# A SwiGLU feed-forward that multiplies its input before the norm factor is known: the factor is applied to the gate and up sums of the first half of the tokens

## The chip, the cores and the metric

The kernel runs on one core of a Trainium2 chip. The time is the device time of one execution in microseconds (us); several executions are timed and the median is taken. One execution more is recorded by the hardware profiler, and the rows in this document come from it. A core has five engines that run their own instruction streams and meet only at semaphores: TensorE (PE, with its weight loads listed as PEld), VectorE (DVE), ScalarE (ACT), GpSimd (POOL) and SyncE (SP), which here only issues DMAs.

## What is computed

The reference is one layer of a decoder with 1,024 prompt tokens and 8 × 4 sample tokens, so 1,056 tokens of width 1,024. What matters here is its end:

```
x = x + (sig(gA) * (A @ w_a) + sig(gB) * (Bn @ w_b)) @ w_o      # the merge; call the new x "x1"
gate, up = split(rmsnorm(x1, g_ffn) @ w_ffn_in)                  # 1024 -> 2 x 2816
x = x1 + (silu(gate) * up) @ w_ffn_out
```

The norm is `rmsnorm(x)[t, d] = x[t, d] * r[t] * g[d]`, where `r[t]` is one over the root of the token's mean square (plus 1e-6). The factor `r[t]` is the same for every channel of a token, so it can be taken out of the product: `gate[t] = r[t] * ((x1 * g) @ w)[t]`, and the same for up.

## The kernel before, in words

Activations lie transposed in SBUF: channels on the 128 partitions, tokens along the free dimension. `x1` is a tile of 8 channel blocks × 1,056 tokens. Every large product is made from three products of rounded parts: a weight block is cast to its high part on ACT (`w_h`), DVE subtracts that from the raw weights (`w_l`), the operand is split in the same way, and `split_product` (L84 to L91) multiplies low × high, high × low and high × high into the same PSUM banks. Each stage is a block of code that all engines leave together: no engine enters the next block before the last one has left the old one.

**The merge** (`stage_merge`, L2423). Its last product, `y @ w_o`, runs in 8 tiles of 128 output channels, each of two weight blocks. Between the two blocks PE transposes the old x for the tile (L2703) from `x_rows`, which POOL has loaded by DMA in four column groups (L2543, L2544) before the product starts. ACT copies the transposed x into `x1` (L2606), DVE adds the product (L2659), ACT squares the tile (`square_tile`, L2600) and POOL adds the squares over the tiles (L2550). ACT and DVE also cast and subtract the weight blocks of the next tile (`split`, L2560, L2622), SP loads them. Behind the last tile stands a chain: ACT squares tile 7, POOL adds it, PE multiplies the sums with a matrix of ones so that every partition has the total of its token (L2709, three pieces of 352 tokens in plain f32), DVE makes the mean square (L2662), ACT the root (L2614), DVE the reciprocal (L2665). That is `k.rs`, the factor r for all 1,056 tokens.

**The feed-forward** (`stage_ffn`, L2712) takes the tokens in two halves of 528. A half has 22 pairs of blocks, gate f and up f (each 8 channel blocks × 6 matmuls of 264 tokens = 48 matmuls), and then 24 blocks of the down product. Weights go raw (three buffers) → `w_h` (ACT, L2830) → `w_l` (DVE, L2890), prepared two blocks ahead (`LEAD`), three deep (`NSPLIT`). At the start of the first half DVE makes each channel block `h2 = x1 * g * r` (`h2_tile`, L2901), ACT its high part `h2_h` (L2834), DVE its low part `h2_l` (L2912), and PE's first block waits for each of the eight in turn. For the second half the same steps run during the down product, with POOL making `h2_l` (L2813). After a gate block ACT takes the Silu out of PSUM (L2866), after the up block DVE multiplies (L2920), ACT casts the result (`act_high`, L2838) and POOL makes its low part (L2818). The order on each engine is that of the program: on ACT, for block n, first the cast of block n+2's weights, then the work of block n; on DVE likewise. PE's gate f waits for the product of pair f-2, whose PSUM banks it takes over.

Of the kernel before, what the change touches and what calls it, by code (L numbers as in the profile page):

```python
# [23 lines left out]
P = 128  # L24
# [2398 lines left out]
def stage_merge(k):  # L2423
# [32 lines left out]
    x_rows = k.at("x_rows", off, [P, TT, DM])  # L2456
    off += TT * DM * 4
    ss = k.at("x1_square_sums", off, [P, TOK])
    square = [k.at(f"x1_square{i}", off + (1 + i) * TOK * 4, [P, TOK]) for i in range(2)]
    assert off + 3 * TOK * 4 <= k.QK_OFF  # L2460
# [24 lines left out]
    s_sq, s_ss, s_tot, s_rs = k.sem("x1_squared"), k.sem("x1_summed"), k.sem("x1_totals"), k.sem("x1_roots")  # L2485
    s_ms = k.sem("x1_mean_squares")
# [16 lines left out]
    with nc.Block() as block:  # L2503
# [31 lines left out]
        def _(pool):  # L2535
# [5 lines left out]
            for i in range(XG):  # L2541
                cols = slice(i * DM // XG, (i + 1) * DM // XG)
                pool.dma_start(x_rows[:, 0:QT, cols], xp[:, :, cols]).then_inc(s_x[i], 16)  # L2543
                pool.dma_start(x_rows[0:NS_TOK, QT, cols], k.x_sample.rearrange("b t d -> (b t) d")[:, cols])\  # L2544
                    .then_inc(s_x[i], 16)
            for f in range(1, KD):
# [6 lines left out]
        def _(act):  # L2553
# [41 lines left out]

            def square_tile(f):
# [5 lines left out]
            for f in range(KD):  # L2602
# [5 lines left out]
                if f:  # L2608
                    square_tile(f - 1)
                split(NM + 2 * f + 1 + LEAD)  # L2610
            square_tile(KD - 1)
            for c in range(NCH):
                act.wait_ge(s_ms, c + 1)
                act.activation(k.rs[:, chunk(c)], k.rs[:, chunk(c)], ACT.Sqrt).then_inc(s_rs, 1)  # L2614

        @block.vector
        def _(dve):
# [15 lines left out]
            for n, (src, _, f) in enumerate(blocks[:NM]):  # L2633
# [4 lines left out]
                if src in "ab":  # L2638
# [5 lines left out]
                    else:  # L2644
# [4 lines left out]
                       .then_inc(s_mul, 1)  # L2649
            for kd in range(KD):  # L2650
                split_operand(y, y_h, y_l, kd, MH + HG + kd)
# [8 lines left out]
            for c in range(NCH):  # L2660
                dve.wait_ge(s_tot, c + 1)
                dve.tensor_scalar(k.rs[:, chunk(c)], ps[:, c, 0:CH], 1.0 / DM, EPS, ALU.mult, ALU.add).then_inc(s_ms, 1)  # L2662
            for c in range(NCH):
                dve.wait_ge(s_rs, c + 1)
                dve.reciprocal(k.rs[:, chunk(c)], k.rs[:, chunk(c)])  # L2665

        @block.tensor
        def _(pe):
# [4 lines left out]
            for n, (src, kt0, f) in enumerate(blocks):  # L2673
# [20 lines left out]
                if src == "o" and kt0 == 0:  # L2694
# [15 lines left out]


def stage_ffn(k):  # L2712
# [7 lines left out]
    raw, s_raw = k.ffn_raw, k.s_ffn_raw  # L2720
    off = k.ROWS_OFF + NRAW * KB * 512
    h2_h, h2_l = (k.at(f"h2_{s}", off + i * KD * HT * 4, [P, KD, HT], F32R) for i, s in enumerate("hl"))
    off += 2 * KD * HT * 4
    act_off = off
    act_h, act_l = (k.at(f"act_{s}", off + i * FT * HT * 4, [P, FT, HT], F32R) for i, s in enumerate("hl"))
    off += 2 * FT * HT * 4
# [3 lines left out]
    assert off <= k.TOP  # L2730
# [13 lines left out]
    for f in range(KD):  # L2744
# [5 lines left out]
    s_t2, s_h2h, s_h2, s_h2b = (k.sem("h2_tile_ready"), k.sem("h2_h_ready"), k.sem("h2_ready_first_half"),  # L2750
                                k.sem("h2_ready_second_half"))
# [454 lines left out]
```

## Time and profile before

| | us |
|---|---|
| median of 3 timed runs | 2223.75 (2218.21 to 2224.26) |
| the profiled execution's own time | 2223.4 |
| its span (first to last instruction) | 2221.5 |
| PE busy in the span | 2018.2 (91%) |
| DVE busy | 1018.9 (46%) |
| ACT busy | 763.3 (34%) |
| POOL busy | 523.8 (24%) |

The time of the execution lies 1.9 us above its span, which runs from the first to the last instruction. The busy shares are averages over stages with different limits. The profile's strip of 40 slices shows PE at 9 tenths from about 1,100 us on, but for the last slice and for one dip to 6 tenths in the slice that begins 1,388 us into the span: there the merge ends and the feed-forward begins.

### The profile page before, as it was taken

How to read it: one execution, taken by the hardware profiler on the slowest of the kernel's cores; microseconds unless marked ns; L12 is line 12 of the kernel's file. 1: busy time of each engine (PE TensorE's matmuls, PEld its weight loads, DVE VectorE, ACT ScalarE, POOL GpSimd, SP SyncE). 2: the span in 40 equal slices, each digit the busy share in tenths (PEclk: the TensorE clock that was granted, in tenths of full speed). 3: DMA queues.
4: the chain of work that ended last, by engine and by line, in shares of the span. 5: the costliest groups of instructions: out<-in, count | busy, mean ns of one | idle time of the engine just before them, and what ended most of it. 6: DMA issues, size and time to landing. Idle time of an engine off the chain costs nothing. (4 is left out here: it accounts for less than half of the span.)

```text
span 2221.5 us, 33109 instructions
## 1 busy us (share of the span) xinstructions
PE 2018.2 (91%) x13796; PEld 1863.1 (84%) x13796; DVE 1018.9 (46%) x1716; ACT 763.3 (34%) x1435; POOL 523.8 (24%) x440
## 2 busy tenths in 40 slices
PE   4999999866888986998899999699999999999997
PEld 3999999855666763665799989599999999999997
DVE  4978863466888873214223243522223223332222
ACT  4232333444766761212222232322222224432212
POOL 1444222104654562222011121111111001111000
PEclk9999999986999987999999999799999999999998
DMA  5455531101000006444433331132323333333332
GB/s 181 140 183 161 164 121 36 39 6 39 1 1 20 1 1 222 141 150 132 157 95 86 90 117 43 49 95 86 95 86 86 95 106 99 99 99 95 86 89 66
DMA packets 258148, 203.11 MB, mean 91 GB/s; under 512 B 20343, under 2 KB 237277, under 8 KB 252688
## 3 DMA queue, kind: packets, MB, share of 16 engines
q1 hardware_dynamic: 246399, 150.92, 23.4%
q0 software_dynamic: 6144, 39.46, 5.2%
q10 hardware_dynamic: 5456, 10.62, 1.5%
q8 instruction: 109, 1.79, 0.3%
q14 instruction: 40, 0.32, 0.0%
HBM read 178.59 MB, written 26.54 MB: 92 GB/s over the span
## 5 line engine op out<-in xcount | busy, mean ns | idle before, releaser
L2890 DVE TENSOR_TENSOR ffn_w_l<-ffn_raw,ffn_w_h 128x1024 fp32r<-128x1024 f32 (+1 forms) x136 | 162.3, 1194 | 345.9 <-ACT ffn_w_h L2830 345.7
L89 PE MATMUL banks<-h_h,ffn_w_l 128*128 128x264 f32 x1408 | 289.0, 287 | 14.1 <-DVE h_l L2912 14.1
L89 PE MATMUL banks<-h_l,ffn_w_h 128*128 128x264 f32 x1408 | 288.6, 286 | 0.0
L89 PE MATMUL banks<-h_h,ffn_w_h 128*128 128x264 f32 x1408 | 288.2, 286 | 0.0
L2830 ACT CAST ffn_w_h<-ffn_raw 128x1024 fp32r<-128x1024 f32 (+1 forms) x136 | 138.7, 1021 | 359.0 <-PE banks L89 352.6
L89 PEld LDWEIGHTS banks<-h_h,ffn_w_l 128*128 128x128 f32 x1408 | 220.0, 189 | 15.6 <-issue 14.2
L89 PEld LDWEIGHTS banks<-h_l,ffn_w_h 128*128 128x128 f32 x1408 | 219.6, 189 | 0.0
L89 PEld LDWEIGHTS banks<-h_h,ffn_w_h 128*128 128x128 f32 x1408 | 219.4, 190 | 0.0
L2818 POOL TENSOR_TENSOR act_l<-ffn_act,act_h 128x528 fp32r<-128x528 f32 x44 | 82.6, 1878 | 478.4 <-ACT act_h L2838 478.4
L89 PE MATMUL banks<-fm_hT_h,fm_w_l 128*128 128x352 f32 x648 | 147.9, 337 | 0.8 <-DVE hT_l L854 0.8
L665 POOL TENSOR_TENSOR fm_w_l<-fm_raw,fm_w_h 128x512 fp32r<-128x512 f32 x54 | 92.0, 1705 | 224.8 <-ACT fm_w_h L722 224.7
L89 PE MATMUL banks<-act_h,ffn_w_l 128*128 128x264 f32 x704 | 142.6, 284 | 0.0
L89 PE MATMUL banks<-act_h,ffn_w_h 128*128 128x264 f32 x704 | 142.5, 283 | 0.0
L89 PE MATMUL banks<-act_l,ffn_w_h 128*128 128x264 f32 x704 | 142.5, 284 | 0.0
L89 PE MATMUL banks<-hT_l,fm_w_h 128*128 128x352 f32 x648 | 141.1, 327 | 0.0
L89 PE MATMUL banks<-fm_hT_h,fm_w_h 128*128 128x352 f32 x648 | 141.0, 326 | 0.0
L1665 POOL TENSOR_SCALAR scores<-scores,row_factor 128x640 f32<-128x640 f32 (+4 forms) x64 | 103.6, 1628 | 113.7 <-DVE row_factor L1869 107.0
L1886 DVE TENSOR_TENSOR probsT_l<-banks,probsT_h 128x512 fp32r<-128x512 f32 (+1 forms) x148 | 100.2, 685 | 39.1 <-ACT probsT_h L1798 37.1
L89 PEld LDWEIGHTS banks<-hT_l,fm_w_h 128*128 128x128 f32 x648 | 112.2, 191 | 0.0
L89 PEld LDWEIGHTS banks<-fm_hT_h,fm_w_h 128*128 128x128 f32 x648 | 111.5, 190 | 0.0
L2622 DVE TENSOR_TENSOR merge_w_l<-merge_raw,merge_w_h 128x512 fp32r<-128x512 f32 x64 | 56.3, 882 | 118.7 <-ACT merge_w_h L2560 118.7
L89 PEld LDWEIGHTS banks<-fm_hT_h,fm_w_l 128*128 128x128 f32 x648 | 107.6, 191 | 2.1 <-DVE hT_l L854 0.9
(507 smaller groups left out, 4184.1 us busy)
## 6 DMA issues: line engine op xcount, KB each, us to landing
ffn_raw<-in_w_ffn_in_dram SPq DMA_DIRECT2D x88, 512.0 KB, 3.9
ffn_raw<-in_w_ffn_out_dram SPq DMA_DIRECT2D x32, 512.0 KB, 3.9
fm_raw<-in_w_in_dram SPq DMA_DIRECT2D x44, 256.0 KB, 3.1
early_w_raw<-in_w_in_dram SPq DMA_DIRECT2D x32, 256.0 KB, 3.0
merge_raw<-in_w_in_dram SPq DMA_DIRECT2D x32, 256.0 KB, 2.8
ffn_raw<-in_w_ffn_out_dram SPq DMA_DIRECT2D x16, 384.0 KB, 3.4
hT_copy<-fm_hT_h SPq DMA_DIRECT2D x4, 1056.0 KB, 6.5
hT_copy<-hT_l SPq DMA_DIRECT2D x4, 1056.0 KB, 5.3
```

Source lines behind the costliest of these rows:

```text
L89: mm = pe.matmul(out[:, bank, 0:cols.stop - cols.start], w[:, kt, :], x[:, kd, cols], start=(first and n == 0), stop=(last and n == 2))
L665: pool.tensor_tensor(w_l[n % NSPLIT][:], raw[n % NRAW][:], w_h[n % NSPLIT][:].bitcast(F32), ALU.subtract)\
L1665: pool.tensor_scalar(s, s, factor[b % 2][:, WINB * HG + i:WINB * HG + i + 1], None, ALU.mult)\
L1886: dve.tensor_tensor(pt_l[x % NPT][0:m, :], ps[0:m, 4 + x % NTB, :], pt_h[x % NPT][0:m, :].bitcast(F32), ALU.subtract).then_inc(s_pl, 1)
L2622: dve.tensor_tensor(w_l[n % NSPLIT][:], raw[n % NRAW][:], w_h[n % NSPLIT][:].bitcast(F32), ALU.subtract)\
L2818: pool.tensor_tensor(act_l[:, f, :], gu[u % 2][:], act_h[:, f, :].bitcast(F32), ALU.subtract)\
L2830: act.copy(w_h[n % NSPLIT][:, 0:m, :], raw[n % NRAW][:, 0:m, :]).then_inc(s_h, 1)
L2890: dve.tensor_tensor(w_l[n % NSPLIT][:, 0:m, :], raw[n % NRAW][:, 0:m, :], w_h[n % NSPLIT][:, 0:m, :].bitcast(F32), ALU.subtract).then_inc( ...
```

## The change

The first half's operand is made without the token factor. During the merge's last product, one tile behind, ACT writes `h2_h = x1 * g` for the first 528 tokens (`h2_high`) and DVE `h2_l = x1 * g - h2_h` (`h2_low`). The chain that makes `k.rs` moves into the feed-forward: ACT squares tile 7 after the casts of the first two weight blocks, POOL adds it there, PE multiplies with the ones right after gate 0 (into banks 4 to 6), DVE and ACT make mean square, root and reciprocal after that (`root`). In the first half DVE multiplies the gate sums with r before the Silu, which ACT now takes from SBUF, and multiplies the Silu with r once more before it multiplies it with the up sums. The second half is as before. To make room, `x_rows` holds two column groups in place of four, so that the third and fourth are loaded when the transposes have left the first and second; tiles are placed elsewhere, and the low parts of the activations lie in two tiles (`split_tiles` is `split_product` with the operand's column block picked by the caller).

```diff
@@ stage_merge @@
-    x_rows = k.at("x_rows", off, [P, TT, DM])
...
+    x_rows = k.at("x_rows", off, [P, 2, TT, DM // 4])
...
@@ stage_merge, gpsimd @@
-            for i in range(XG):
+            def rows(i):
                 cols = slice(i * DM // XG, (i + 1) * DM // XG)
...
+                if i >= 2:
+                    pool.wait_ge(s_xt, 6 * (i - 1))
+                pool.dma_start(x_rows[:, i % 2, 0:QT, :], xp[:, :, cols]).then_inc(s_x[i], 16)
...
-            for f in range(1, KD):
+            rows(0)
+            rows(1)
+            for f in range(1, KD - 1):
+                if f in (1, 3):
+                    rows(2 + f // 2)
                 pool.wait_ge(s_sq, f + 1)
...
@@ stage_merge, scalar @@
+            def h2_high(f):
+                act.wait_ge(s_x1, f + 1)
+                act.activation(k.h2[0][:, f, :], k.x1[:, f, 0:HT], ACT.Copy,
+                               scale=k.cols[:, k.c_norm_ffn + f:k.c_norm_ffn + f + 1]).then_inc(s_h2h, 1)
...
                 if f:
+                    h2_high(f - 1)
                     square_tile(f - 1)
                 split(NM + 2 * f + 1 + LEAD)
-            square_tile(KD - 1)
-            for c in range(NCH):
-                act.wait_ge(s_ms, c + 1)
-                act.activation(k.rs[:, chunk(c)], k.rs[:, chunk(c)], ACT.Sqrt).then_inc(s_rs, 1)
+            h2_high(KD - 1)
@@ stage_merge, vector @@
+            def h2_low(f):
+                dve.wait_ge(s_h2h, f + 1)
+                dve.scalar_tensor_tensor(k.h2[1][:, f, :], k.x1[:, f, 0:HT],
+                                         k.cols[:, k.c_norm_ffn + f:k.c_norm_ffn + f + 1],
+                                         k.h2[0][:, f, :].bitcast(F32), ALU.mult, ALU.subtract)
...
                 dve.tensor_tensor(x1, x1, banks(product[n]), ALU.add).then_inc(s_x1, 1)
-            for c in range(NCH):
-                dve.wait_ge(s_tot, c + 1)
-                dve.tensor_scalar(k.rs[:, chunk(c)], ps[:, c, 0:CH], 1.0 / DM, EPS, ALU.mult, ALU.add).then_inc(s_ms, 1)
-            for c in range(NCH):
-                dve.wait_ge(s_rs, c + 1)
-                dve.reciprocal(k.rs[:, chunk(c)], k.rs[:, chunk(c)])
+                if f:
+                    h2_low(f - 1)
+            h2_low(KD - 1)
@@ stage_merge, tensor @@
-            pe.wait_ge(s_x1, KD)
-            pe.wait_ge(s_ss, KD - 1)
-            for c in range(NCH):
-                pe.matmul(ps[:, c, 0:CH], k.ones[:], ss[:, chunk(c)], start=True, stop=True).then_inc(s_tot, 1)
@@ stage_ffn, gpsimd @@
+            pool.wait_ge(k.s_sq, KD)
+            pool.wait_ge(k.s_ss, KD - 2)
+            pool.tensor_tensor(k.ss[:], k.ss[:], k.square[(KD - 1) % 2][:], ALU.add).then_inc(k.s_ss, 1)
...
@@ stage_ffn, scalar @@
             for n in range(LEAD):
                 split(n)
-            for kd in range(KD):
-                h2_tile(kd)
+            act.wait_ge(k.s_ss, KD - 3)
+            act.activation(k.square[(KD - 1) % 2][:], k.x1[:, KD - 1, :], ACT.Square).then_inc(k.s_sq, 1)
...
                     if f:
                         act_high(u - 1)
-                    act.wait_ge(s_used, n + 1)
-                    if u >= 2:
+                    if n == 0:
+                        for c in range(NCH):
+                            act.wait_ge(s_ms, c + 1)
+                            act.activation(k.rs[:, chunk(c)], k.rs[:, chunk(c)], ACT.Sqrt).then_inc(s_root, 1)
+                    if hf == 0:
+                        act.wait_ge(s_gs, u + 1)
+                        act.activation(gu[u % 2][:], gu[u % 2][:], ACT.Silu).then_inc(s_silu, 1)
+                    else:
+                        act.wait_ge(s_used, n + 1)
                         act.wait_ge(s_al, u - 1)
-                    act.activation(two(gu[u % 2][:]), pair(4 * (f % 2)), ACT.Silu).then_inc(s_silu, 1)
+                        act.activation(two(gu[u % 2][:]), pair(4 * (f % 2)), ACT.Silu).then_inc(s_silu, 1)
...
@@ stage_ffn, vector @@
-            h2_tile(0, 0)
-            for kd in range(KD):
-                if kd + 1 < KD:
-                    h2_tile(0, kd + 1)
-                dve.wait_ge(s_h2h, kd + 1)
-                dve.tensor_tensor(h2_l[:, kd, :], h2[kd % 2][:], h2_h[:, kd, :].bitcast(F32), ALU.subtract)\
-                   .then_inc(s_h2, 1)
+            def root():
+                for c in range(NCH):
+                    dve.wait_ge(s_tot, c + 1)
+                    dve.tensor_scalar(k.rs[:, chunk(c)], ps[:, 4 + c, 0:CH], 1.0 / DM, EPS, ALU.mult, ALU.add)\
+                       .then_inc(s_ms, 1)
+                for c in range(NCH):
+                    dve.wait_ge(s_root, c + 1)
+                    dve.reciprocal(k.rs[:, chunk(c)], k.rs[:, chunk(c)]).then_inc(s_rs, 1)
+                dve.wait_ge(s_rs, NCH)
+
+            link = Chain(dve, s_chain)
             for n, (hf, src, kt, m, f) in enumerate(blocks):
                 split(n + LEAD)
                 u = FT * hf + f
+                if src == "gate" and hf == 0:
+                    if f == 0:
+                        root()
+                    dve.wait_ge(s_used, n + 1)
+                    if u >= 2:
+                        dve.wait_ge(s_al, u - 1)
+                    dve.tensor_tensor(two(gu[u % 2][:]), pair(4 * (f % 2)), two(k.rs[:, 0:HT]), ALU.mult).then_inc(s_gs, 1)
                 if src == "up":
                     dve.wait_ge(s_silu, u + 1)
+                    if hf == 0:
+                        link(dve.tensor_tensor(gu[u % 2][:], gu[u % 2][:], k.rs[:, 0:HT], ALU.mult))
...
@@ stage_ffn, tensor @@
+                    if src == "gate" and f == 1 and hf == 0:
+                        pe.wait_ge(s_ms, NCH)
...
                 for kt in range(m):
-                    if src == "gate" and f == 0:
-                        pe.wait_ge(s_h2b if hf else s_h2, kt + 1)
+                    if src == "gate" and f == 0 and hf:
+                        pe.wait_ge(s_h2b, kt + 1)
...
                 mm.then_inc(s_used, 1)
+                if n == 0:
+                    pe.wait_ge(k.s_ss, KD - 1)
+                    for c in range(NCH):
+                        pe.matmul(ps[:, 4 + c, 0:CH], k.ones[:], k.ss[:, chunk(c)], start=True, stop=True).then_inc(s_tot, 1)
```

## Rows read from the trace of the kernel before

**Rows 1.** Stretches of the span: busy us (instructions) per engine, granted clock, DMA share, GB/s
```profile
1402.00:1435.00 33.00, 18.95 (x112) 16.84 (x111) 24.88 (x27) 13.32 (x19) 0.00 (x0) 0.68 0.23 65
...
1446.00:1560.00 114.00, 114.00 (x934) 114.00 (x933) 31.23 (x30) 31.08 (x40) 18.28 (x10) 1.00 0.31 89
```

**Rows 2.** Timeline, all engines, merge's end to FFN's second block: start us, us, instruction [idle before]
```profile
1395.06 0.65 PE L89 MATMUL banks<-y_h,merge_w_h 128*128 128x352 f32 x3
1395.74 1.25 DVE L2659 TENSOR_TENSOR x1T<-x1T,banks 128x1056 f32<-128x1056 f32 x1 [11.92 <-PE banks L89]
1397.03 1.08 ACT L2600 ACTIVATE x_square<-x1T 128x1056 f32<-128x1056 f32 x1 [5.84 <-DVE x1T L2659]
...
1398.19 2.40 POOL L2550 TENSOR_TENSOR x_square_sums<-x_square_sums,x_square 128x1056 f32<-128x1056 f32 x1 [4.45 <-ACT x_square L2600]
...
1400.74 3.86 PE L2709 MATMUL banks<-x_square_sums,ones 128*128 128x352 f32 x6 [5.04 <-POOL x_square_sums L2550]
...
1405.08 6.77 DVE L2665 RECIPROCAL x_rstd<-x_rstd 128x352 f32<-128x352 f32 x3
...
1412.12 1.99 ACT L2830 CAST ffn_w_h<-ffn_raw 128x1024 fp32r<-128x1024 f32 x2 [6.43 <-PEq L2503]
1413.20 2.36 DVE L2890 TENSOR_TENSOR ffn_w_l<-ffn_raw,ffn_w_h 128x1024 fp32r<-128x1024 f32 x2 [1.35 <-ACT ffn_w_h L2830]
...
1416.94 0.71 DVE L2912 TENSOR_TENSOR h_l<-h_tile,h_h 128x528 fp32r<-128x528 f32 x1
...
1417.79 0.78 PE L89 MATMUL banks<-h_h,ffn_w_l 128*128 128x264 f32 x2 [13.19 <-DVE h_l L2912]
...
1418.37 0.65 PE L89 MATMUL banks<-h_l,ffn_w_h 128*128 128x264 f32 x2
...
1418.81 0.65 PE L89 MATMUL banks<-h_h,ffn_w_h 128*128 128x264 f32 x2
...
1427.19 1.28 ACT L2866 ACT_TABLE_LOAD   x1
...
1427.87 0.41 PE L89 MATMUL banks<-h_h,ffn_w_l 128*128 128x264 f32 x2
```

**Rows 3.** Stretches, columns as in Rows 1, around the idle and the restart
```profile
1395.00:1399.00 4.00, 0.70 (x5) 0.41 (x3) 1.25 (x1) 1.95 (x2) 0.81 (x1) 1.00 0.00 0
...
1417.75:1423.00 5.25, 5.21 (x22) 5.16 (x23) 5.14 (x8) 2.15 (x4) 0.00 (x0) 0.50 0.35 101
```

**Rows 4.** One line's instructions each: min/median/max ns, first and last start
```profile
L2901 DVE SCALAR_TENSOR_TENSOR h_tile<-x1T,vector_cols,x_rstd x16: 760/764/1832, 1415.5 to 1794.3; 128x528 f32<-128x528 f32 x16
...
L2834 ACT CAST h_h<-h_tile x16: 632/632/636, 1416.3 to 1795.1; 128x528 fp32r<-128x528 f32 x16
...
L2920 DVE TENSOR_TENSOR ffn_act<-ffn_act,banks x44: 703/704/706, 1434.0 to 2072.1; 128x528 f32<-128x528 f32 x44
```

**Rows 5.** Timelines of ACT, DVE and POOL, one pair of gate and up
```profile
1545.53 0.61 ACT L2866 ACTIVATE ffn_act<-banks 128x528 f32<-128x528 f32 x1 [4.24 <-PE banks L89]
1546.04 1.04 ACT L2830 CAST ffn_w_h<-ffn_raw 128x1024 fp32r<-128x1024 f32 x1
...
1547.12 1.23 DVE L2890 TENSOR_TENSOR ffn_w_l<-ffn_raw,ffn_w_h 128x1024 fp32r<-128x1024 f32 x1 [5.09 <-ACT ffn_w_h L2830]
...
1553.12 1.83 POOL L2818 TENSOR_TENSOR act_l<-ffn_act,act_h 128x528 fp32r<-128x528 f32 x1 [9.92 <-ACT act_h L2838]
```

**Rows 6.** Timelines of DVE and POOL at the first half's end
```profile
1682.42 1.83 DVE L2901 SCALAR_TENSOR_TENSOR h_tile<-x1T,vector_cols,x_rstd 128x528 f32<-128x528 f32 x1
...
1682.14 1.55 POOL L2818 TENSOR_TENSOR act_l<-ffn_act,act_h 128x528 fp32r<-128x528 f32 x1 [9.72 <-ACT act_h L2838]
```

**Rows 7.** Timelines of ACT and DVE in the merge's last product; its DMA issues
```profile
1349.34 1.16 ACT L2606 COPY x1T<-banks 128x512 f32<-128x512 f32 x3 [10.00 <-PE banks L2703]
...
1351.05 0.69 DVE L2622 TENSOR_TENSOR merge_w_l<-merge_raw,merge_w_h 128x512 fp32r<-128x512 f32 x1 [6.72 <-ACT merge_w_h L2560]
...
x_rows<-in_x_prompt_dram POOLq DMA_DIRECT2D x4, 1024.0 KB, 9.4
```

More of the change, by code:

```diff
@@ L89, in split_product, with split_tiles @@
             mm = pe.matmul(out[:, bank, 0:cols.stop - cols.start], w[:, kt, :], x[:, kd, cols],
+                           start=(first and n == 0), stop=(last and n == 2))
+    return mm
+def split_tiles(pe, out, w_h, w_l, kt, x_h, x_l, pieces, first, last):
+    for n, (w, x) in enumerate(((w_l, x_h), (w_h, x_l), (w_h, x_h))):
+        for bank, cols in pieces:
+            mm = pe.matmul(out[:, bank, 0:cols.stop - cols.start], w[:, kt, :], x[:, cols],
                            start=(first and n == 0), stop=(last and n == 2))
@@ L2455, in stage_merge @@
     off = k.ROWS_OFF + FFN_RAW * KD * 512
-    x_rows = k.at("x_rows", off, [P, TT, DM])
[L2457 to L2460, printed above, removed]
+    x_rows = k.at("x_rows", off, [P, 2, TT, DM // 4])
+    off += 2 * TT * DM
+    HT = TOK // 2
+    ss = k.ss = k.at("x1_square_sums", k.SPARE2_OFF + TOK * 4, [P, TOK])
+    square = k.square = [k.at("x1_square0", off, [P, TOK]), k.at("x1_square1", k.SPARE2_OFF + 2 * TOK * 4, [P, TOK])]
+    k.H2_OFF = off + 3 * TOK * 4
+    assert k.H2_OFF + 2 * KD * HT * 4 <= k.QK_OFF and k.SPARE2_OFF + 3 * TOK * 4 <= k.HB_OFF
+    k.h2 = [k.at(f"h2_{part}", k.H2_OFF + i * KD * HT * 4, [P, KD, HT], F32R) for i, part in enumerate("hl")]
     XG = 4
@@ L2720, in stage_ffn @@
     raw, s_raw = k.ffn_raw, k.s_ffn_raw
+    h2_h, h2_l = k.h2
+    FL = 3
     off = k.ROWS_OFF + NRAW * KB * 512
[L2722 to L2726, printed above, removed]
     w_h = [k.at(f"ffn_w_h{i}", off + 2 * i * KB * 512, [P, KB, P], F32R) for i in range(NSPLIT)]
@@ L2729, in stage_ffn, with act_low @@
     off += 2 * NSPLIT * KB * 512
-    assert off <= k.TOP
+    act_l_first = k.at("act_l_first", off, [P, FL, HT], F32R)
+    assert off + FL * HT * 4 <= k.H2_OFF
+    off = act_off = k.H2_OFF + 2 * KD * HT * 4
+    act_h = k.at("act_h", off, [P, FT, HT], F32R)
+    act_l_rest = k.at("act_l_rest", off + FT * HT * 4, [P, FT - FL, HT], F32R)
+    assert off + (2 * FT - FL) * HT * 4 <= k.TOP
+    def act_low(f):
+        return act_l_first[:, f, :] if f < FL else act_l_rest[:, f - FL, :]
     off = k.SPARE2_OFF + TOK * 4
@@ L2755, in stage_ffn @@
     EARLY = HT // XT
-    late = [act_off + (i * FT + FT - 4) * HT * 4 for i in range(2)]
+    late = [act_off + (FT - 4) * HT * 4, act_off + (2 * FT - FL - 4) * HT * 4]
     e_rows = [k.at(f"early_rows{i}", late[i], [P, DM]) for i in range(2)]
@@ L2779, in pair, with chunk @@
         return ps[:, bank:bank + 2, 0:HC]
+    def chunk(c):
+        return slice(c * CH, (c + 1) * CH)
     def two(t):
@@ L2817, in _ @@
                     pool.wait_ge(s_ah, u + 1)
-                    pool.tensor_tensor(act_l[:, f, :], gu[u % 2][:], act_h[:, f, :].bitcast(F32), ALU.subtract)\
+                    pool.tensor_tensor(act_low(f), gu[u % 2][:], act_h[:, f, :].bitcast(F32), ALU.subtract)\
                         .then_inc(s_al, 1)
@@ L2880, in _ @@
                     if hf == 0:
-                        h2_tile(KD + f)
+                        h2_tile(f)
         @block.vector
@@ L2959, in _ @@
                     first_bank = down_bank(f)
-                    x_h, x_l = act_h, act_l
+                    x_h, x_l = act_h, act_low
                 else:
+                    if src == "gate" and f == 1 and hf == 0:
+                        pe.wait_ge(s_ms, NCH)
                     if src == "gate" and f >= 2:
```

27 lines of the change are left out of this document (13 added, 14 removed).

## The prediction

> **What bounds the kernel now.** I read the profile's page first: PE is busy for 91% of the span, so time can only be won where PE stands still or runs slowly. The busy times by stretch then say where. In the feed-forward proper PE is busy for all of 114.00 us at the full granted clock, 934 matmuls, 0.122 us each; in the 33 us between 1402 and 1435 it is busy for 18.95 us at a mean clock of 0.68 [rows 1]. So what matters is that border, and its timeline is the third view [rows 2]. Read it as one chain. PE's last matmul of the merge ends at 1395.06 + 0.65 = 1395.71. DVE adds the last tile until 1396.99; ACT squares it, POOL adds it until 1400.59, PE makes the totals (3.86), DVE, ACT and DVE make the factor, and the last reciprocal ends at 1411.85. Only then do all engines leave the merge: ACT's first cast of feed-forward weights starts at 1412.12, although it had nothing else to do. DVE's first subtraction follows at 1413.20, and then come three more dependent steps for the first channel block, up to h_l at 1417.65. PE restarts at 1417.79, 22.1 us after it stopped. It also restarts slowly: the granted clock was still 1.00 in the four us to 1399, and is 0.50, which is 1.2 GHz, from 1417.75 to 1423 [rows 3]. Two matmuls are then 0.44 apart (1418.37 to 1418.81) [rows 2], 0.22 each. The block of up 0 begins at 1427.87, so gate 0 took 10.08 us against 48 × 0.122 = 5.86 at the full clock.
>
> A measurement of this kernel can tell about 0.3%, 6.7 us, from no change.
>
> **The change, part by part.** I rebuild the chain up to the start of up 0, because from there on PE was never idle before.
>
> *The merge's tail.* DVE ends the last addition at 1396.99 as before. Behind it now stand h2_low(6) and h2_low(7). They are three-operand instructions on 128x528 like h_tile, 0.764 each [rows 4]. h2_high(7) on ACT runs beside h2_low(6): the nearest cast is 0.632 [rows 4]; a scale per channel may add some 0.1, and it still ends by 1397.8. So h2_low(7) ends at about 1398.55. The chain of squares, sum, totals, root and reciprocals is gone from here: the reciprocals ended at 1411.85, so the engines leave 13.3 us earlier. The next block begins 0.27 after the last engine, as before (1411.85 to 1412.12): 1398.82.
>
> *The entry.* ACT's cast to DVE's subtraction took 1.08, and one subtraction takes 1.23 [rows 2, 5]: the first low weights are ready at 1398.82 + 1.08 + 1.23 = 1401.13. PE started 0.14 behind its last operand before, so now at 1401.27. All eight channel blocks lie ready; before, the first was another 3 us of steps. PE's start is 16.5 us earlier.
>
> *Gate 0.* The idle time shrinks from 22.1 to 5.6 us, but the clock had fallen within 5 us (1.00 to 1399, 0.50 before 1400.74, when the totals ran: three pieces in 3.86) [rows 2, 3]. I take a cold start, as before. The cold stretch before was at least the 5.25 us of its row; I take 5.5. Then 25 matmuls cost 5.5 and the other 23 cost 23 × 0.122 = 2.8: 8.3 us, to 1409.57. The bounds are 5.86 (never cold) and 48 × 0.22 = 10.56 (cold throughout). I take 8.3 because the only restart of the same matmuls in the trace rose after that time. Gate 0 also stops waiting for DVE: before, DVE delivered a channel block every 1.4 us, which is what used up the rest of the 10.08.
>
> *Totals on PE's path.* They now stand between gate 0 and up 0. At the half clock they took 3.86 [rows 2]; PE is at work before them, so half of that, 1.93. The upper bound is 3.86, the lower 1.7 (the last result's way out is in the 1.93). Their operand: ACT's two casts end at 1400.8, the square of tile 7 takes 1.08, POOL's addition 2.40 [rows 2], ready at about 1404.4, five us before gate 0 ends. Hidden by gate 0; if gate 0 were never cold it ends at 1407.1 and still hides it. Up 0 begins at 1409.57 + 1.93 = 1411.5.
>
> *The factor.* It is now needed by DVE's scaling of gate 0, and PE can run on through up 0, gate 1 and up 1 meanwhile. But behind `root` DVE has w_l of up 1 in its queue, and ACT has that block's cast behind the Silu of gate 0. Before, totals to last reciprocal took 1411.85 - 1400.74 = 11.11; less 1.93 for the faster totals, 9.2. Then scaling 0.70 (L2920 is the nearest row, one operand in PSUM [rows 4]), Silu 0.61, cast 1.04, subtraction 1.23 [rows 5], and some 0.25 for the handshakes: 13.0 after gate 0. PE wants it after totals, up 0 and gate 1: 1.93 + 11.7 = 13.65. It fits with 0.6 us to spare; I cost it at nothing, and anything by which it is longer than that is paid in full. ACT changes tables to Sqrt and Silu; each load is 1.28 [rows 2], the first beside gate 0, the second beside the 6.77 us of reciprocals.
>
> *The pairs of the first half.* 22 scalings and 22 second multiplications on DVE, 0.70 each [rows 4], some 31 us of DVE in a stretch where it waits 5.09 us in front of one subtraction [rows 5]. Within a pair the chain is cast 1.04, subtraction 1.23, scaling 0.70, Silu 0.61, cast 1.04, subtraction 1.23, two multiplications 1.41 and the next cast of act_h 0.63: 7.9, with handshakes 8.4, against 11.7 of PE per pair. Hidden; without that cover each us over 11.7 would cost 22 us.
>
> *The merge's last product.* Per tile ACT gets 0.63 to 0.75 and DVE 0.76 more; ACT waits 10.00 in front of a tile's copies and DVE 6.72 in front of a subtraction [rows 7], and the weight blocks queued behind them are for the next tile. Nothing. The four x DMAs that move behind transposes of tiles 1 and 3 are issued by POOL between its additions, land 9.4 us later [rows 7], and are wanted three tiles of 13.2 us after their release. Nothing; SP's queue is untouched.
>
> **Sum.** Up 0 starts at 1411.5 in place of 1427.87: 16.4 us earlier, and all after it is unchanged. The profiled execution took 2223.4, so 2207.0; the median of the runs is 0.35 above that execution, which makes 2207.4. I say **2207**.
>
> **The rivals.**
>
> *The clock never falls* in the shorter gap. For it: 1.00 held for 3.3 us of idling, to 1399 [rows 3]; the new gap is 5.6. Against it: the clock was down by 1400.74, 5 us into the idle time. Gate 0 then takes 5.86: 2.4 us more are won, 2204.6. Chance 0.19.
>
> *The new start is longer than I built it*: the weights of up 1 come late behind `root`, or the totals are slower. The 0.6 us of slack are thin; a table load that isn't hidden (1.28) costs 0.7, totals at the half clock 1.9, both with one more handshake chain some 4 in all. 2208 to 2211. Chance 0.16.
>
> *The early start doesn't come off.* The profile puts PE's wait in front of gate 0 down to h_l, but what an engine needs to begin a new block is hidden by those 13.19 us [rows 2]; were it some 10 us or more, almost all would be lost: about 2217 to 2223, no change. Against it: ACT began 0.27 after the last engine. Chance 0.05.
>
> *Slower: the pair chain becomes the bound.* Its place is DVE's and ACT's loop over the 22 pairs. A DVE instruction with two SBUF inputs took 1.83 where its median is 0.764, beside a POOL subtraction [rows 4, 6]: held, it costs 1.07 more. Four such holds per pair would make 8.4 into 12.7, 1.0 us over PE's 11.7, and 22 × 1.0 = 22 against a gain of 16.4: 2229 and more. It decides from a chain of 12.5 per pair on (16.4 / 22 = 0.75 over). Against it: POOL has one instruction of 1.83 per pair [rows 5] and can hold one DVE instruction, not four. Chance 0.04. The Trainium skill (GPSIMD Engine Reference, Specifications) says that GpSimd's SBUF interfaces are shared with VectorE and contend with VectorE instructions that have two SBUF inputs, which the second multiplication is; by that rule alone the pairs would lengthen. The trace agrees that there is such a hold, with its 1.83.
>
> **How the numbers follow.** The forecast itself has 0.56, with a range of its own of 2204 to 2210. It, the clock that stays up and the longer start all lie over 0.3% below: 0.56 + 0.19 + 0.16 = 0.91 faster. Within 0.3%: 0.05. Slower: 0.04. The range must take in 2204.6 and 2211; the runs before lay between 2218.2 and 2224.3, that is 5.5 below and 0.5 above their median. So 2200 to 2213, which leaves out the two last rivals and the tails.
>
> **What would show it.** Right: no L2709 or reciprocals before the last engine leaves the merge; PE idle for about 5.6 us; gate 0's matmuls without waits on DVE, 0.22 apart and then 0.122; totals of about 1.9 us in front of up 0; PE without a gap to the end. Wrong: a PE gap in front of up 1 (waiting for ffn_w_l) shows the factor on the path; gaps in front of gates 2 to 21 waiting for ffn_act or ffn_w_l show the pair chain; idle time of PE in the merge's tiles shows the moved x loads or casts; a PE restart long after the first ffn_w_l shows the entry cost.

## The result, and the profile after

The changed kernel takes **2207.45 us** (median of four runs, 2205.3 to 2208.72); the kernel before, run beside it, 2223.75 (2218.21 to 2224.26). The ratio is **0.9929**, with an interval of 0.9911 to 0.9947: 16.3 us, or 0.7%, faster. Forecast were 2207 and a range of 2200 to 2213.

The profiled executions took 2223.4 before and 2205.3 after, 18.1 apart. The first matmul of the merge's last product starts 2.1 us earlier in the second one (1285.63 against 1287.70); all before it is unchanged code, so I take that as a difference of the two executions and no gain: one execution more of the changed kernel (the last experiments) reaches that product's end at 1398.35, this one at 1393.62. I therefore compare from the end of that product on, and call the stretch from there to the start of up 0 **the border**.

The page of the changed kernel: the parts on busy time and on the costliest group of PE that waits.

```profile
PE 2016.2 (92%) x13796; PEld 1862.3 (85%) x13796; DVE 1045.0 (47%) x1752; ACT 764.2 (35%) x1435; POOL 527.9 (24%) x440
...
L98 PE MATMUL banks<-h_h,ffn_w_l 128*128 128x264 f32 x1408 | 288.3, 286 | 5.5 <-DVE ffn_w_l L2933 5.5
```

Behind the second bar stands the idle time of PE in front of that whole group: 5.5 us over all gate and up blocks, all of it for ffn_w_l. DVE has 26.1 us more to do than before (1045.0 against 1018.9), and no wait of PE comes of it.

The border in the timeline of the changed kernel (start us, us, instruction, idle time before it and what ended it):

```profile
1392.97 0.65 PE L89 MATMUL banks<-y_h,merge_w_h 128*128 128x352 f32 x3
1393.66 1.25 DVE L2688 TENSOR_TENSOR x1T<-x1T,banks 128x1056 f32<-128x1056 f32 x1 [11.24 <-PE banks L89]
1394.83 1.66 DVE L2675 SCALAR_TENSOR_TENSOR h_l<-x1T,vector_cols,h_h 128x528 fp32r<-128x528 f32 x2
...
1396.76 1.99 ACT L2866 CAST ffn_w_h<-ffn_raw 128x1024 fp32r<-128x1024 f32 x2 [1.08 <-PEq L2515]
1397.84 2.36 DVE L2933 TENSOR_TENSOR ffn_w_l<-ffn_raw,ffn_w_h 128x1024 fp32r<-128x1024 f32 x2 [1.35 <-ACT ffn_w_h L2866]
...
1399.12 0.81 PE L98 MATMUL banks<-h_h,ffn_w_l 128*128 128x264 f32 x2 [5.50 <-DVE ffn_w_l L2933]
...
1399.82 2.69 POOL L2844 TENSOR_TENSOR x_square_sums<-x_square_sums,x_square 128x1056 f32<-128x1056 f32 x1 [7.75 <-ACT x_square L2879]
...
1400.71 2.88 DVE L2933 TENSOR_TENSOR ffn_w_l<-ffn_raw,ffn_w_h 128x1024 fp32r<-128x1024 f32 x1 [0.51 <-ACT ffn_w_h L2866]
...
1407.50 1.94 PE L3037 MATMUL banks<-x_square_sums,ones 128*128 128x352 f32 x6
1408.29 1.71 DVE L2950 TENSOR_SCALAR x_rstd<-banks 128x352 f32<-128x352 f32 x3 [4.71 <-PE banks L3037]
...
1409.01 0.67 PE L98 MATMUL banks<-h_h,ffn_w_l 128*128 128x264 f32 x2
...
1409.92 6.77 DVE L2954 RECIPROCAL x_rstd<-x_rstd 128x352 f32<-128x352 f32 x3
1410.01 0.40 PE L98 MATMUL banks<-h_h,ffn_w_l 128*128 128x264 f32 x2
...
1416.72 0.71 DVE L2967 TENSOR_TENSOR ffn_act<-banks,x_rstd 128x528 f32<-128x528 f32 x1
...
1419.08 1.23 DVE L2933 TENSOR_TENSOR ffn_w_l<-ffn_raw,ffn_w_h 128x1024 fp32r<-128x1024 f32 x1 [1.65 <-ACT ffn_w_h L2866]
...
1420.99 0.41 PE L98 MATMUL banks<-h_h,ffn_w_l 128*128 128x264 f32 x2
```

The rows that answer to [rows 2]: PE stops at 1393.62 and gate 0 starts at 1399.12, 5.50 later, all of it idle, where it had been 22.08 (18.22 idle and 3.86 for the totals). The square, the sum and the totals now lie beside gate 0 or behind it, the reciprocals beside up 0 and gate 1. The totals take 1.94 where they took 3.86, and up 0 starts 1.51 after their start. It starts a little slowly: its first six matmuls take 1.00 (1409.01 to 1410.01), where up 0 took 0.72 for them before. Up 0 as a whole takes 6.10 in place of 5.87, so 0.23 more belongs to the price of the totals. The row at 1420.99 is the start of up 1.

Stretches of the span (PE, PEld, DVE, ACT and POOL busy with their instructions, granted clock, DMA share, GB/s):

```profile
1393.60:1397.50 3.90, 0.02 (x1) 0.00 (x0) 2.70 (x3) 1.48 (x2) 0.00 (x0) 1.00 0.00 0
1397.50:1398.00 0.50, 0.00 (x0) 0.00 (x0) 0.16 (x1) 0.50 (x2) 0.00 (x0) 0.74 0.13 33
1399.10:1404.50 5.40, 5.38 (x24) 5.38 (x25) 3.98 (x2) 2.86 (x3) 2.69 (x1) 0.50 0.72 194
1404.50:1409.00 4.50, 4.50 (x32) 3.97 (x31) 0.64 (x2) 0.15 (x1) 0.00 (x0) 0.99 0.40 117
...
1400.00:1720.00 320.00, 320.00 (x2596) 319.37 (x2596) 126.82 (x135) 86.70 (x108) 47.46 (x27) 0.99 0.32 91
```

The clock did fall within the shorter gap too: 1.00 to 1397.5, 0.74 in the half microsecond after it, 0.50 (1.2 GHz) for the first 24 matmuls of gate 0, then full. The last row is the one that the pairs rest on: once started, PE is busy for 320.00 of 320 us.

| the border, us | before | after |
|---|---|---|
| last product's end to gate 0 | 22.08 | 5.50 |
| gate 0 | 10.08 | 8.38 |
| totals on PE's path | (in the first row) | 1.51 |
| last product's end to up 0 | 32.16 | 15.39 |
| up 0 to the execution's last instruction | 793.63 | 794.29 |

So the border gives 16.77 us, 16.54 of it left at the start of gate 1. Of the 0.66 that the rest is longer, 0.23 is up 0's slower start; the other 0.4 I leave unexplained. It is no more than executions differ there: in the kernels below with the moved chain and no extra work behind up 0, that rest takes 792.8 to 794.2.

### The profile page after: what moved, and what is told of

Same layout as the page of the kernel before. It is cut to its first block and busy times, and to the rows that moved or that the text cites. A ratio compares the mean times of both kernels' runs of the same rounds, so it can differ in the third digit from the quotient of the medians.

```text
span 2203.3 us, 33142 instructions
## 1 busy us (share of the span) xinstructions
PE 2016.2 (92%) x13796; PEld 1862.3 (85%) x13796; DVE 1045.0 (47%) x1752; ACT 764.2 (35%) x1435; POOL 527.9 (24%) x440
## 5 line engine op out<-in xcount | busy, mean ns | idle before, releaser
L2854 POOL TENSOR_TENSOR act_l_rest<-ffn_act,act_h 128x528 fp32r<-128x528 f32 x38 | 71.3, 1876 | 377.3 <-ACT act_h L2874 377.3
L674 POOL TENSOR_TENSOR fm_w_l<-fm_raw,fm_w_h 128x512 fp32r<-128x512 f32 x54 | 96.5, 1788 | 218.4 <-ACT fm_w_h L731 218.4
L98 PE MATMUL banks<-act_l_rest,ffn_w_h 128*128 128x264 f32 x608 | 123.2, 284 | 0.0
L98 PEld LDWEIGHTS banks<-act_h,ffn_w_h 128*128 128x128 f32 x704 | 109.2, 189 | 0.0
```

The lines of the kernel that those rows point to most:

```text
L674: pool.tensor_tensor(w_l[n % NSPLIT][:], raw[n % NRAW][:], w_h[n % NSPLIT][:].bitcast(F32), ALU.subtract)\
L2854: pool.tensor_tensor(act_low(f), gu[u % 2][:], act_h[:, f, :].bitcast(F32), ALU.subtract)\
```

## The experiments

The changed kernel has two parts that can be undone one at a time: the norm's **chain** leaves the path in front of gate 0, and the **operand** is made early, within the merge. The first two kernels undo one part each. The next two put a load on the pairs, the fifth on the factor, and the last ones work on what is left of the border. The borders are read from the profiled executions; they tell more than medians where less than 5 us matter, since executions of one kernel scatter by 4 us and more. All borders are counted to the start of up 0; where the totals stand in front of it, 0.23 of their price lies behind that point.

### The chain stays at the merge's end

The operand without the factor is made within the merge as in the changed kernel, but squares, totals, root and reciprocals are where they were before.

```diff
@@ stage_merge, tensor @@
+            pe.wait_ge(s_x1, KD)
+            pe.wait_ge(s_ss, KD - 1)
+            for c in range(NCH):
+                pe.matmul(ps[:, c, 0:CH], k.ones[:], ss[:, chunk(c)], start=True, stop=True).then_inc(s_tot, 1)
@@ stage_merge, vector; likewise the root on scalar and the square on scalar and gpsimd @@
+            for c in range(NCH):
+                dve.wait_ge(s_rs, c + 1)
+                dve.reciprocal(k.rs[:, chunk(c)], k.rs[:, chunk(c)])
@@ stage_ffn, vector @@
-                    if f == 0:
-                        root()
```

> The changed kernel with one part undone: squares, sum, totals, root and reciprocals stay at the merge's end; the operand without the factor and the scaling in the pairs stay as changed. Theory (the chain is most of the gain): the engines leave the merge 16.1 us after the last x1 addition starts (1395.74 to 1411.85 before) in place of 2.8 (1393.66 to 1396.5), 13.3 later; the totals (1.5 between gate 0 and up 0 in the changed kernel) go off PE's path again. So 11.8 us slower than the changed kernel's 2207.5: 2219.3, 4.5 us faster than before. Rival (making the operand within the merge is what gains): 2207 to 2210.

Measured: 2219.22 us, 0.9976 (0.9963 to 0.999) of the kernel before, which took 2225.21 beside it. The profiled execution took 2211.57, less than the median, and reaches the product's end early (1390.17); the border is counted from there. Its timeline:

```profile
1389.52 0.65 PE L89 MATMUL banks<-y_h,merge_w_h 128*128 128x352 f32 x3
...
1391.38 0.76 DVE L2680 SCALAR_TENSOR_TENSOR h_l<-x1T,vector_cols,h_h 128x528 fp32r<-128x528 f32 x1
...
1392.66 2.41 POOL L2571 TENSOR_TENSOR x_square_sums<-x_square_sums,x_square 128x1056 f32<-128x1056 f32 x1 [4.04 <-ACT x_square L2626]
...
1393.24 2.39 DVE L2680 SCALAR_TENSOR_TENSOR h_l<-x1T,vector_cols,h_h 128x528 fp32r<-128x528 f32 x1 [1.10 <-ACT h_h L2619]
...
1399.55 6.76 DVE L2702 RECIPROCAL x_rstd<-x_rstd 128x352 f32<-128x352 f32 x3
...
1408.95 0.81 PE L98 MATMUL banks<-h_h,ffn_w_l 128*128 128x264 f32 x2 [9.88 <-DVE ffn_w_l L2938]
...
1416.98 0.41 PE L98 MATMUL banks<-h_h,ffn_w_l 128*128 128x264 f32 x2
```

From the product's end (1390.17) to the last reciprocal's (1406.31) it is 16.14 us, to the hundredth what it was before (1395.71 to 1411.85, [rows 2]). Only what follows is shorter: PE restarts 2.64 after the reciprocals (before 5.94), and gate 0, no longer fed one channel block at a time, takes 8.03 (before 10.08). The border is 26.81. So with the chain in its old place the early operand, made without the factor, is worth 5.35 of the 16.77 us, and **the other 11.42 are the chain's**: 13.28 less between the product and gate 0, 0.35 more in gate 0, and 1.51 for the totals on PE's path.

### The operand is made at the feed-forward's start

Here the chain is where the change puts it, but the sixteen instructions that make the operand stand behind the first weights.

```diff
@@ stage_merge, scalar and vector @@
-                    h2_high(f - 1)
-            h2_high(KD - 1)
...
-                    h2_low(f - 1)
-            h2_low(KD - 1)
@@ stage_ffn, scalar, behind the first two casts; the low parts likewise on vector @@
+            for kd in range(KD):
+                act.activation(h2_h[:, kd, :], k.x1[:, kd, 0:HT], ACT.Copy,
+                               scale=k.cols[:, k.c_norm_ffn + kd:k.c_norm_ffn + kd + 1]).then_inc(s_uh, 1)
@@ stage_ffn, tensor @@
+                    if src == "gate" and f == 0:
+                        pe.wait_ge(s_h2b if hf else s_ul, kt + 1)
```

> The changed kernel with the other part undone: the first half's operand without the factor is made at the start of the feed-forward, by the same two instructions per channel block, behind the first two weight blocks; the chain stays moved and the pairs scale as changed. Theory (without the factor the operand needs no place in the merge): no h2_low pair at the merge's end (1.66 less), but one more weight subtraction (1.2) and one h2_low (0.76) in front of PE's restart, then 0.8 per channel block against 1.31 of six matmuls at the half clock: the restart comes 0.3 later, 2207.8, the same as the changed kernel; up to 1.5 more if POOL's last addition, now behind eight casts on ACT (about 6 us later), ends after gate 0. Rival (the operand's steps at the entry were worth their 3.2 us and gate 0's waits for DVE, 10.08 against 8.4): 2212.

Measured: 2206.88 us, 0.9925 (0.99 to 0.9949), the same as the changed kernel. Its timeline:

```profile
1394.91 0.65 PE L89 MATMUL banks<-y_h,merge_w_h 128*128 128x352 f32 x3
...
1401.40 0.78 PE L98 MATMUL banks<-h_h,ffn_w_l 128*128 128x264 f32 x2 [5.85 <-DVE h_l L2948]
...
1405.20 3.12 POOL L2840 TENSOR_TENSOR x_square_sums<-x_square_sums,x_square 128x1056 f32<-128x1056 f32 x1 [11.61 <-ACT x_square L2878]
...
1406.09 3.31 DVE L2932 TENSOR_TENSOR ffn_w_l<-ffn_raw,ffn_w_h 128x1024 fp32r<-128x1024 f32 x1
...
1411.18 0.67 PE L98 MATMUL banks<-h_h,ffn_w_l 128*128 128x264 f32 x2
```

PE is idle for 5.85 in place of 5.50, and the border is 15.62 in place of 15.39. What the early operand saves at the start, it costs at the merge's end: there the two low parts behind the last addition take 1.66 before any engine may leave. The two parts of the change thus don't add up, and the four borders say it best: 32.16 with neither (the kernel before), 26.81 with the early operand alone, 15.62 with the moved chain alone, 15.39 with both. **The moved chain alone gives 16.54 of the 16.77 us**; making the operand early is worth 0.2 once the chain is gone. What both rest on is that the factor has been taken out of the product; no run here takes it out and leaves both parts undone, so what that alone is worth isn't shown. This kernel keeps the halved x_rows.

### More work on DVE in each pair

Six and ten extra multiplications of 128x528 stand in front of each scaling of the gate sums from gate 3 on, 19 pairs. Their result is not read.

```diff
+            pad = Chain(dve, k.sem("padding"))
...
+                    for _ in range(6 if f >= 3 else 0):
+                        pad(dve.tensor_tensor(h2[0][:], k.rs[:, 0:HT], k.rs[:, 0:HT], ALU.mult))
```

> The changed kernel with six more multiplications of 128x528 on DVE (0.70 each and a handshake, 4.2 to 4.7 in all) in front of the scaling of each gate from gate 3 on; they write a scratch tile. By the prediction's sum of the pair chain, 8.4, it becomes 12.6 to 13.1 against 11.74 of PE: 0.9 to 1.3 more for 19 pairs, 17 to 25 us, 2225 to 2232. Rival (the chain that must close within a pair is shorter: scaling, Silu, cast, subtraction, two multiplications and the next subtraction, 6.4, since the casts of the next gate and of act_h run beside it): 10.6 to 11.1, hidden, 2207.5.

> As with six more multiplications per pair, now ten. With six, DVE's loop over a pair had 1.15 us of idle time left, in front of the first extra one: the loop takes 10.6 of 11.75, 0.74 per extra one. With ten it takes 13.55, 1.8 over PE's pair. Theory (the pair chain decides from this loop's length on, 6.2 without extras): 19 pairs times 1.8 is 34, less what the blocks prepared ahead absorb at first (some 5 to 9): 25 to 29 more, 2232 to 2236. Rival (the sum of 8.4 that the prediction made): with ten, 8.4 + 7.4 = 15.8, 4.1 over, 78 more: 2285.

Measured: with six 2206.24 us, 0.9918 (0.9894 to 0.9942), no cost; with ten 2260.77 us, 1.0165 (1.014 to 1.019), 53 more than the changed kernel. DVE's timeline, one pair, in the changed kernel:

```profile
1550.40 0.71 DVE L2967 TENSOR_TENSOR ffn_act<-banks,x_rstd 128x528 f32<-128x528 f32 x1 [3.51 <-PE banks L98]
...
1556.34 0.70 DVE L2973 TENSOR_TENSOR ffn_act<-ffn_act,banks 128x528 f32<-128x528 f32 x1 [1.74 <-PE banks L98]
```

with six extras:

```profile
1550.39 4.42 DVE L2969 TENSOR_TENSOR h_tile<-x_rstd 128x528 f32<-128x528 f32 x6 [1.15 <-PE banks L98]
...
1562.07 4.42 DVE L2969 TENSOR_TENSOR h_tile<-x_rstd 128x528 f32<-128x528 f32 x6 [1.15 <-PE banks L98]
```

and with ten:

```profile
1558.00 0.71 DVE L2970 TENSOR_TENSOR ffn_act<-banks,x_rstd 128x528 f32<-128x528 f32 x1
1560.35 1.22 DVE L2933 TENSOR_TENSOR ffn_w_l<-ffn_raw,ffn_w_h 128x1024 fp32r<-128x1024 f32 x1 [1.65 <-ACT ffn_w_h L2866]
...
1563.99 8.54 DVE L2969 TENSOR_TENSOR h_tile<-x_rstd 128x528 f32<-128x528 f32 x10
1572.56 0.71 DVE L2970 TENSOR_TENSOR ffn_act<-banks,x_rstd 128x528 f32<-128x528 f32 x1
```

The bracket is the reading. In the changed kernel DVE waits for PE twice per pair, 3.51 and 1.74. With six extras one wait of 1.15 is left in a round of 11.68, so the loop itself takes 10.5, and without the six (4.45) **6.1**. With ten no wait for PE is left: from scaling to scaling it is 14.56, and then DVE sets the pace. 14.56 − 11.68 = 2.88 per pair, × 19 = 55, against 53 measured. I had expected 25 to 29 there, because I took 0.74 for each extra. The ten took 8.54 and not 7.4. The extras' line in that kernel (min, median and max of one, in ns) says why:

```profile
L2969 DVE TENSOR_TENSOR h_tile<-x_rstd x190: 707/709/1854, 1448.7 to 1717.3; 128x528 f32<-128x528 f32 x190
```

The median is 709 and the longest 1854: beside POOL's act_l, one of the ten is held for some 1.15. In 18 of the 19 pairs the ten take 8.51 to 8.54 (in the first, 7.40); that makes 21 us, most of what the expectation lacked. The mechanism of the rival is real, but the changed kernel has 5.6 us per pair of room below it.

### The reciprocals three times

```diff
-                for c in range(NCH):
-                    dve.wait_ge(s_root, c + 1)
-                    dve.reciprocal(k.rs[:, chunk(c)], k.rs[:, chunk(c)]).then_inc(s_rs, 1)
-                dve.wait_ge(s_rs, NCH)
+                for rep in range(3):
+                    for c in range(NCH):
+                        dve.wait_ge(s_root, c + 1)
+                        dve.reciprocal(k.rs[:, chunk(c)], k.rs[:, chunk(c)]).then_inc(s_rs, 1)
+                    dve.wait_ge(s_rs, NCH * (rep + 1))
```

An odd number of reciprocals leaves the same factor. The kernel was timed like the others, and run once more for its profile.

> The changed kernel with the reciprocals of the factor taken three times in a row (which gives the reciprocal again), 13.5 us more on DVE in the chain from totals to factor. Theory (from 0.4 us on, in the profile of the changed kernel, each us of this chain stands on PE's path in front of up 1 and is never caught up): PE waits 13.1 us in front of up 1, the time is 2207.5 + 13.1 = 2220.6, or some 2 us more if the clock falls in that wait. Rival (PE makes it up, or the chain is hidden by more than up 0 and gate 1): 2207 to 2212.

> The kernel with the reciprocals taken three times, once more for an undisturbed profile. Its runs took 2223.4, 16.7 more than the changed kernel, where 13.1 or some 2 more was expected. Theory: PE waits 13.1 in front of up 1 for ffn_w_l, and the clock falls in that wait, so that up 1 starts with a cold stretch as gate 0 does (2.5). Rival: there is a second wait, behind up 1, since act_h and the weights of gate 2 are late too.

Measured: 2223.44 us, 0.9997 (0.9987 to 1.0007); the single run 2223.37. All of the gain is gone. PE's two waits and the reciprocals in the timeline of the single run:

```profile
1401.31 0.81 PE L98 MATMUL banks<-h_h,ffn_w_l 128*128 128x264 f32 x2 [5.49 <-DVE ffn_w_l L2933]
...
1436.27 0.81 PE L98 MATMUL banks<-h_h,ffn_w_l 128*128 128x264 f32 x2 [12.86 <-DVE ffn_w_l L2933]
```

```profile
1412.22 20.39 DVE L2955 RECIPROCAL x_rstd<-x_rstd 128x352 f32<-128x352 f32 x9
```

13.6 us more of reciprocals give a wait of 12.86 in front of up 1. Counted by starts, up 1 begins 24.96 after up 0 (1411.31) in place of 11.98, 13.0 later, so 0.6 of the reciprocals were hidden: that is the slack, measured from the other side. The timeline of the changed kernel gives 0.7: w_l of up 1 ends at 1420.31, and PE gets to it at 1420.99. The clock falls in that wait as well: up 1 takes 8.14 where 48 matmuls take 5.86 at the full clock, 2.3 more. By starts, both together are some 15.2 of the 16.0 by which the medians differ.

### What is left of the border

Four kernels: the changed kernel once more; unread matmuls over PE's idle time (16 behind the merge's last product, 15 in front of gate 0); the first two weight blocks of the feed-forward split during the merge's last tile; and both together (16 and 1 unread matmuls).

```diff
@@ unread matmuls: stage_merge and stage_ffn, tensor @@
+            pe.wait_ge(s_xt_copied, 3 * KD)
+            for _ in range(16):
+                pe.matmul(ps[:, 7, 0:CH], y_h[:, 0, 0:P], y_h[:, 0, 0:CH], start=True, stop=True)
...
+            for _ in range(15):
+                pe.matmul(ps[:, 7, 0:HC], h2_h[:, 0, 0:P], h2_h[:, 0, 0:HC], start=True, stop=True)
@@ early weights: stage_merge, scalar; the subtraction likewise on vector @@
+                if f == KD - 1:
+                    for i in range(2):
+                        act.wait_ge(k.s_ffn_raw[i], 16)
+                        act.copy(k.fw_h[i][:], k.ffn_raw[i][:]).then_inc(k.f_h, 1)
@@ early weights: stage_ffn, scalar and vector @@
-            for n in range(LEAD):
-                split(n)
```

> The changed kernel once more, without an edit, as the one that the three kernels beside it are compared with: 2207.5 within 0.2%, and PE's own idle time at the border 5.5 us.

> The changed kernel with matmuls whose results nobody reads in PE's idle time at the border: 16 of 352 columns behind the merge's last product, 15 of 264 in front of gate 0. Theory (the cold stretch of gate 0 comes from the idle time alone and costs 8.38 - 5.86 = 2.5 us): the granted clock stays at 1.00 from the merge into gate 0, gate 0 takes 5.9, the time is 2.5 less: 2205.0. Rival (gate 0 is slow for another reason, or the idle time isn't what lowers the clock): 2207.5, with 24 matmuls of gate 0 still 0.22 apart.

> The changed kernel with the high and low parts of the first two weight blocks of the feed-forward made during the merge's last tile, on ACT and DVE in front of the last tile's sum. Theory (PE's restart hangs on the engines leaving the merge plus cast 1.08 and subtraction 1.23): PE restarts about 0.3 after the last engine leaves, 2.3 earlier: 2205.2; the idle time is then some 3.2 us in place of 5.5, and if the clock stays up in it, 2.5 less again: 2202.7. Rival (what stands behind the restart is an entry cost of PE, or the extra work in the last tile delays the merge's end): 2207 or more.

> Both together, with 16 matmuls for nobody behind the merge's product and 1 in front of gate 0. If the two gains are of different kinds (2.3 of idle time, 2.5 of clock) they add: 2202.7. If the early weights alone keep the clock up, the same as early weights alone.

| us | median | ratio to before | PE idle | gate 0 | border |
|---|---|---|---|---|---|
| changed, again | 2206.72 | 0.992 (0.9902 to 0.9937) | 5.50 | 8.4 | 15.42 |
| unread matmuls | 2205.14 | 0.9917 (0.9898 to 0.9936) | 0.88 | 5.97 | 12.98 |
| early weights | 2204.88 | 0.9911 (0.9893 to 0.9928) | 3.17 | 7.45 | 12.12 |
| both | 2203.37 | 0.9907 (0.9889 to 0.9925) | 0.60 | 5.85 | 10.72 |

PE's timeline with the unread matmuls:

```profile
1397.55 2.73 PE L2734 MATMUL banks<-y_h 128*128 128x352 f32 x16
1400.88 2.05 PE L3005 MATMUL banks<-h_h 128*128 128x264 f32 x15 [0.60 <-PEq L2515]
1403.21 0.51 PE L98 MATMUL banks<-h_h,ffn_w_l 128*128 128x264 f32 x2 [0.28 <-DVE ffn_w_l L2936]
...
1409.18 1.94 PE L3042 MATMUL banks<-x_square_sums,ones 128*128 128x352 f32 x6
```

```profile
1403.20:1409.20 6.00, 5.99 (x49) 5.99 (x50) 3.99 (x2) 2.86 (x3) 2.70 (x1) 1.00 0.65 187
```

Gate 0 starts 5.50 after the product's end, as in the changed kernel, and runs at a granted clock of 1.00. It takes 5.97 in place of 8.4: the cold start costs **2.4 us**, the price that the prediction gave the clock that stays up. With the early weights, PE's restart and the stretches around it (columns as above):

```profile
1402.17 0.49 PE L98 MATMUL banks<-h_h,ffn_w_l 128*128 128x264 f32 x2 [3.17 <-PEq L2518]
```

```profile
1402.00:1402.50 0.50, 0.33 (x3) 0.36 (x4) 0.00 (x0) 0.35 (x1) 0.00 (x0) 1.00 0.00 0
1402.50:1403.00 0.50, 0.50 (x6) 0.50 (x5) 0.00 (x0) 0.50 (x1) 0.00 (x0) 0.92 0.00 0
1403.00:1403.50 0.50, 0.50 (x5) 0.50 (x4) 0.00 (x0) 0.50 (x2) 0.19 (x1) 0.50 0.36 88
1405.50:1406.00 0.50, 0.50 (x4) 0.50 (x4) 0.50 (x1) 0.00 (x0) 0.26 (x1) 0.50 1.16 331
1406.00:1406.50 0.50, 0.50 (x5) 0.50 (x5) 0.50 (x1) 0.00 (x0) 0.00 (x0) 0.67 1.21 293
1406.50:1407.00 0.50, 0.50 (x6) 0.50 (x6) 0.35 (x1) 0.00 (x0) 0.00 (x0) 1.00 0.70 166
```

2.33 us of the idle time go, and 0.96 of gate 0: the border falls by 3.3. The unread matmuls alone took 2.4 off it, both edits together take 4.7, to 10.72. So the two edits' gains don't quite add, since the earlier start already saves a part of the cold one; what adds is the idle time, 2.3, and the cold start, 2.4. The medians differ by 1.6, 1.8 and 3.3 us from the changed kernel's, less than its executions scatter (2205.23 to 2209.43), and their intervals overlap: the order of these kernels rests on the borders.

## Why the prediction was right

The time is 0.45 us from the forecast, less than two executions of one kernel differ; with executions that scatter by 4 us so close a hit is in part luck. What bears the forecast out is the border, where no term of the sum was off by more than about 0.4. Times are counted from the end of the merge's last product, so that the two executions can be compared.

| us | predicted | measured |
|---|---|---|
| engines enter the feed-forward | 3.11 | 3.14 |
| PE restarts | 5.56 | 5.50 |
| gate 0 | 8.3 | 8.38 |
| totals on PE's path | 1.93 | 1.51, and 0.23 in up 0 |
| up 0 starts | 15.8 | 15.39 |
| w_l of up 1 ready, after gate 0's end | 13.0 | 12.8 |
| slack of the factor | 0.6 | 0.7 |
| gain on the border | 16.4 | 16.77 to up 0, 16.54 to gate 1 |

*The merge's tail and the entry.* As built. The casts with a scale per channel took 0.736 to 0.761, the plain cast 0.632 [rows 4]; I had allowed "some 0.1". The Trainium skill (ScalarE: Activation LUTs, What ACT_TABLE_LOAD costs) states that each pointer operand of one element per partition adds about 93 ns; the trace agrees, with 0.104 to 0.129, and 0.086 where the casts were shortest (0.718, in the first two experiments).

*Gate 0.* The cold start came, and 24 matmuls at the half clock took 5.4 where 25 in 5.5 were assumed.

*Totals.* **This term was slightly too large**: half of 3.86, 1.93, is their time from first start to last end (1.94 measured), and I put all of it in front of up 0. Up 0 starts 1.51 after their start, below the lower bound of 1.7, but its own start then takes 0.23 longer. Together that is 1.74 on PE's path, 0.2 less than forecast and within the bounds.

*The factor.* It has the slack that it was given, and the reciprocals three times show that it is real and thin: 0.6 to 0.7 us, and everything over it was paid.

*The pairs.* Hidden, as forecast, but **the sum of 8.4 for the pair chain was wrong**; it is 6.1. I put one of ACT's two weight casts and its cast of act_h into one chain with DVE's work, and they run beside it: with ten extras, w_l begins 2.35 after the scaling, and then DVE goes through its four instructions without a stop, 3.64, up to the next extras. The rival that ends on the other side thus stood further away than its 12.5 against 8.4 said. Its condition was right: with ten extras the loop passed PE's 11.7, and the kernel became slower than before.

*The merge's last product.* From its first matmul to its last it took 108.01 before and 107.99 after: the sixteen instructions and the moved loads of x cost nothing there.

*The rivals.* The clock did fall, so the first did not come; the unread matmuls show that its price, 2.4, was right. The longer start and the lost start did not come: ACT's first cast begins at 1396.76, 0.27 after DVE's last low part, as between the stages before. As to the holds, the reading behind the fourth rival is confirmed in other places: beside POOL's addition, w_l took 2.88 and 3.31 where it takes 1.23, and a low part 2.39 where it takes 0.76. The Trainium skill (GPSIMD Engine Reference, Specifications) names exactly this, instructions of VectorE with two SBUF inputs; the trace agrees, and adds that here the held instruction ended with POOL's or later. In the border that hold stood beside gate 0, and cost nothing.

*Which part carries the gain.* The prediction didn't ask. The first two experiments do: the moved chain, with the factor taken out, gives 16.5 us by itself, the early operand 0.2 on top of it.

## What to carry to other kernels

A factor that is the same for a whole row of the product can go behind the product: what it takes to make it can then lie beside the matmuls, and all that counts is the first consumer's date (here the start of up 1, 13.5 us after gate 0's end, with some 0.7 to spare). Before the making of an operand is moved into an earlier stage as well, count what it adds to that stage's end: here it cost there nearly what it saved. At a border that PE waits through, look at the idle time and the cold start as two prices: here an early start took 2.3 off the first (and, alone, 1.0 off the second), filler matmuls the whole 2.4 of the second, and both together 4.7.

## What the runs showed of the hardware that I had not expected

The clock can fall after PE is at work again. With the early weights PE was idle for 3.17 us, restarted at 1402.17 with the clock at 1.00, and kept it for most of the next half microsecond (0.92 in 1402.50 to 1403.00). The granted clock was then 0.50 from 1403.00 to 1406, with PE busy throughout, and gate 0 took 7.45 in place of 5.85. The shorter gap alone didn't keep the full clock; filling it did.

A DVE instruction with two inputs in SBUF that began beside a GpSimd addition was, in these rows, not slowed in part but ended only after it: in the border of the changed kernel, POOL's addition ran until 1402.51 and w_l, begun at 1400.71, until 1403.59, 1.08 after it, most of its own 1.23. The low part in the first experiment ended 0.56 after POOL's addition (1395.63 and 1395.07). Where the DVE instruction had begun first, it was the GpSimd one that took longer: in the changed kernel's pairs, w_l begins at 1545.66 and takes its usual 1.22, and POOL's act_l, begun beside it at 1546.24, takes 1.86; where less of the two lies side by side, with ten extras, act_l takes 1.60 (1563.68).
